# Two model blocks on one core: an extra turn at the norms' links of the branches, second buffers for bonus and gate, the first level of the inverses first, and VectorE copies over two PSUM banks

## The chip, the cores and the metric

One core of one Trainium2 chip runs the whole kernel in one launch. The metric is the device time in microseconds, the median of several runs. The engines are TensorE (PE in the profile, its weight loads PEld), VectorE (DVE), ScalarE (ACT), GpSimd (POOL) and the DMA queue of SyncE (SP). They run their own instruction streams and meet at semaphores.

## The reference, cut to what matters

Two blocks in float32 on 256 tokens of width 2048. The first block has two layers of mixed attention (stage L of the kernel). The second is one layer with a context of 256 tokens (stage P projects the inputs, stage C merges and runs the MLP). Between P and C lie the two branches, stage B, which the diff is about. Branch a is an RWKV-7 scan in both directions with 16 heads of 64, branch b a gated delta rule in both directions with 8 heads of 128.

```python
# branch a, each direction: S_t = S_{t-1} diag(w_t) - (S_{t-1} kk_t) b_t^T + v_t k_t^T ; y_t = S_t r_t
kk = l2_normalize(heads(k * k_k))
mean = jnp.mean(y, -1); var = jnp.mean(jnp.square(y - mean), -1)
out = (((y - mean) * rsqrt(var + eps)) * ln_w + ln_b + bonus) * gate     # bonus = sum_d (r k_d r_k) * v
# branch b, each direction, in chunks:
q = l2_normalize(q) * B_HEAD ** -0.5; k = l2_normalize(k)
a_mat = tril(kb @ k.T * decay, -1) + eye                                  # solved for u, w
out = o * rsqrt(mean(o * o) + eps) * norm_w * silu(gz)
```

## The kernel before, in words

Both scans are run in chunks of 128 tokens, four to a direction (the tokens of the input and of the context). A chunk needs the inverse of a unit triangular matrix. It is built by doubling: level 0 takes 2x2 blocks, level 5 blocks of 64, and a last step joins two of 64 to one of 128. X holds the inverse so far, XP its transpose, NA the matrix. A level has two links: TensorE multiplies NA by X (event `iq`), VectorE masks the result into Q; TensorE multiplies Q by XP and by itself (event `it`), and ScalarE and VectorE copy the new X and XP out of PSUM. `inverse_a` does this for eight 128-blocks (branch a, two heads by four chunks), `inverse` for four (branch b).

Stage B is a weave: eight streams (`thread_a(0)`, `thread_b(0)`, `thread_a(1)`, `thread_b(1)`, `tail_a`, `tail_b`, `base_a`, `base_b`) are generators; each engine runs its own version of all eight and takes one step, up to the next `yield`, of each in this order. One pass over the eight is a turn here. A `yield` makes no instruction: it sets only where in an engine's queue the next ones stand. Since an engine's queue is in order, a wait holds all that stands behind it. A thread's tile goes through `prep`, `scores`, the inverse and `chain` (branch a; b has its own four steps), which is 34 turns for both, eight tiles a direction. Direction 1 starts a tile when direction 0 is 8 turns into its inverse (`middle`, `middleb`). `base_a` and `base_b` prepare the next tile (mixes, convolutions, l2 norms of kk, q and k), `tail_a` and `tail_b` finish one (group norm of y and the gate; RMS norm of o).

A norm is a row of links: ScalarE squares (`sq`), TensorE sums over channels (`sums`), VectorE scales the sums (`mean`, by `ts` or `root`), GpSimd takes the power (`root`, L3226), TensorE spreads the result (`spread`), VectorE multiplies.

Lines in the profile: L574 is the `mm` helper of TensorE, L577 its transpose, L1417 and L1420 the two helpers of ScalarE (activation, copy), L2153 VectorE's `ts`. The others stand for themselves: L2734 (X and XP from the identity), L2742 (masked copies into XP), L2747 (first level of X) in `inverse_a`, L2759 its Q, L2764 and L2765 its copies; L2687 to L2703 the same in `inverse`; L2855 and L2863 the masked copies of `scores` into NA, AK, RB and RK; L2953 and L2956 thread_b's matrix, L2608 the mix for the next tile of a. PSUM is eight banks of 512 float32 a partition; branch a's direction d uses banks 2d and 2d+1 in turn (`Ring` d0, d1), the norms banks 6 and 7 (`bs`).

## Time and profile before

| | |
|---|---|
| median of 3 runs | 3774.3 us (3773.59 to 3777.36) |
| profiled execution | 3773.41 us, span 3771.5 us |
| TensorE busy | 3575.4 us, 95% of the span |
| VectorE busy | 2224.6 us, 59% |
| ScalarE, GpSimd busy | 1521.8 us, 1651.4 us |
| mean granted TensorE clock | 0.975 |
| stage B | about 1891.5 to 2822 us |
| in it, cycle of 34 turns | 107 us |

A busy engine is one that has an instruction under way; matmuls are pipelined, and their ends are modelled. The idle time in front of an instruction is put down to what released it.

### The profile page before, as it was taken

The numbers are of one execution on the slowest core, as the hardware profiler recorded it, in microseconds if no ns is written. First come the engines' busy times: TensorE is split into PE (matmuls) and PEld (weight loads), VectorE is DVE, ScalarE is ACT, GpSimd is POOL, SyncE is SP. The second block draws the span as 40 slices with busy tenths as digits, with TensorE's granted clock in tenths as the row PEclk, the third lists the DMA queues.
The fourth block names the chain that finished last, engine by engine and source line by source line (L and its number), as shares of the span: only waits on it lengthen the run. The fifth ranks groups of instructions, "written<-read, shape, count | busy, mean of one in ns | idle before, by whom it ended". The sixth has DMA issues, their size and how long they took to land. (4 is left out here: it accounts for less than half of the span.)

```text
span 3771.5 us, 79181 instructions
## 1 busy us (share of the span) xinstructions
PE 3575.4 (95%) x33504; PEld 3118.9 (83%) x33504; DVE 2224.6 (59%) x4232; ACT 1521.8 (40%) x2753; POOL 1651.4 (44%) x1195
## 2 busy tenths in 40 slices
PE   7999998999997999999979999999979999999998
PEld 6888787888786888888868878888869898989897
DVE  4645535655536776677666677666656654445443
ACT  4444434444435432232223333333334453535353
POOL 5555455555554543333321111111116566666664
PEclk9999999999999999999989999999999999999999
DMA  6445554444344777778610000000006445455543
GB/s 229 183 168 189 186 196 156 178 179 181 146 176 168 257 268 257 252 257 292 215 40 18 24 28 29 25 24 15 3 33 254 174 179 190 179 190 180 188 180 134
DMA packets 116368, 586.83 MB, mean 156 GB/s; under 512 B 20912, under 2 KB 40368, under 8 KB 51376
## 3 DMA queue, kind: packets, MB, share of 16 engines
q1 hardware_dynamic: 116016, 581.76, 42.2%
q8 instruction: 267, 4.37, 0.5%
q14 instruction: 85, 0.70, 0.1%
HBM read 561.00 MB, written 20.71 MB: 154 GB/s over the span
## 5 line engine op out<-in xcount | busy, mean ns | idle before, releaser
L574 PE MATMUL bank<-act_L,part_L 128*128 128x512 f32 (+1 forms) x4864 | 935.4, 347 | 9.2 <-DMA cst<-in_cst 4.8
L574 PEld LDWEIGHTS bank<-act_L,part_L 128*128 128x128 f32 x4864 | 756.1, 191 | 146.4 <-issue 28.1
L574 PE MATMUL bank<-act_P,part_P 128*128 128x512 f32 (+1 forms) x3488 | 716.4, 365 | 17.5 <-POOL part_P L3221 12.6
L3221 POOL TENSOR_TENSOR part_C<-wring,part_C 128x512 fp32r<-128x512 f32 x320 | 567.8, 1783 | 362.3 <-ACT part_C L1420 362.3
L3221 POOL TENSOR_TENSOR part_L<-wring,part_L 128x512 fp32r<-128x512 f32 x304 | 526.2, 1732 | 446.1 <-ACT part_L L1420 438.2
L574 PEld LDWEIGHTS bank<-act_P,part_P 128*128 128x128 f32 x3488 | 590.3, 188 | 136.9 <-DVE arena_P L2590 16.1
L574 PE MATMUL bank<-arena_B 64*64 64x64 f32 (+2 forms) x11200 | 446.0, 237 | 51.1 <-DVE arena_B L2747 24.8
L3221 POOL TENSOR_TENSOR part_P<-wring,part_P 128x512 fp32r<-128x512 f32 x184 | 306.3, 1670 | 427.7 <-ACT part_P L1420 427.7
L1420 ACT ACTIVATE part_C<-wring 128x1024 fp32r<-128x1024 f32 x320 | 338.0, 1057 | 347.9 <-PE bank L574 345.7
L574 PE MATMUL bank<-act_Y,part_C 128*128 128x258 f32 (+1 forms) x3840 | 464.8, 283 | 9.4 <-POOL part_C L3221 9.4
L574 PEld LDWEIGHTS bank<-act_Y,part_C 128*128 128x128 f32 x3840 | 463.9, 191 | 9.8 <-issue 9.6
L574 PEld LDWEIGHTS bank<-arena_B 64*64 64x64 f32 (+2 forms) x11200 | 380.7, 147 | 103.5 <-DVE arena_B L2747 27.2
L574 PE MATMUL bank<-act_C,part_C 128*128 128x512 f32 (+1 forms) x2560 | 459.6, 340 | 0.0
L574 PEld LDWEIGHTS bank<-act_C,part_C 128*128 128x128 f32 x2560 | 391.6, 188 | 58.0
L1420 ACT ACTIVATE part_L<-wring 128x1024 fp32r<-128x1024 f32 x304 | 320.7, 1056 | 255.6 <-PE bank L574 255.0
L2167 DVE TENSOR_TENSOR part_L<-wring,part_L 128x512 fp32r<-128x512 f32 x304 | 248.2, 816 | 254.7 <-ACT part_L L1420 253.5
L2167 DVE TENSOR_TENSOR part_C<-wring,part_C 128x512 fp32r<-128x512 f32 x320 | 235.0, 734 | 252.2 <-ACT part_C L1420 245.4
L2167 DVE TENSOR_TENSOR part_P<-wring,part_P 128x512 fp32r<-128x512 f32 x184 | 170.1, 925 | 189.9 <-ACT part_P L1420 189.8
L2228 DVE SCALAR_TENSOR_TENSOR arena_P<-arena_P,mods 128x512 f32<-128x512 f32 x240 | 272.7, 1136 | 8.9 <-DMA arena_P<-in_w 5.5
L1420 ACT ACTIVATE part_P<-wring 128x1024 fp32r<-128x1024 f32 x184 | 190.9, 1051 | 153.1 <-PE bank L574 152.4
L574 PE MATMUL bank<-wring,arena_B 64*64 64x64 f32 (+3 forms) x2208 | 193.1, 254 | 7.5 <-DVE arena_B L2855 3.1
L3358 POOL COPY arena_B<-cst 128x256 f32<-128x256 f32 x80 | 33.3, 416 | 379.1 <-PE bank L574 379.1
(262 smaller groups left out, 3595.1 us busy)
## 6 DMA issues: line engine op xcount, KB each, us to landing
wring<-in_w SPq DMA_DIRECT2D x404, 1024.0 KB, 4.9
arena_P<-in_w SPq DMA_DIRECT2D x64, 1024.0 KB, 5.2
mring<-in_w SPq DMA_DIRECT2D x32, 1024.0 KB, 6.6
z_kept<-arena_P SPq DMA_DIRECT2D x34, 256.0 KB, 5.7
z_kept<-arena_P SPq DMA_DIRECT2D x58, 128.0 KB, 5.6
xT<-z_kept SPq DMA_DIRECT2D x26, 256.0 KB, 2.7
arena_C<-z_kept SPq DMA_DIRECT2D x32, 128.0 KB, 2.8
cst<-z_kept SPq DMA_DIRECT2D x24, 128.0 KB, 2.1
```

Of the source, the lines that this page charges most:

```text
L574: return e.matmul(out, lhsT, rhs, start=start, stop=stop)
L1420: return e.activation(out, a, ACT.Copy, scale=scale)
L2167: tt(wl[:, 0:4, :], wring[s % NS][:, 8 * j:8 * j + 4, :], wh[:, 0:4, :].bitcast(F32), sub).then_inc(*mark("dve_lo", "lov", stage, h))
L2228: z = ts(a, x, c, None, mult, None) if row == 0 else stt(a, x, c, a, mult, add)
L3221: e.tensor_tensor(wl[:, 4:8, :], wring[s % NS][:, 8 * j + 4:8 * j + 8, :], wh[:, 4:8, :].bitcast(F32), sub).then_inc(*mark("pool_lo", "lop ...
L3358: e.tensor_copy(region(Q[lv % 2], wd, d), same).then_inc(*mark(sem, "qf", tag, lv))
```

## The change

- All eight banks become one PSUM tensor; `banks[i]` is a slice of it, so an access may span the two banks of a direction (`two_banks(d)`).
- `scores` on VectorE: NA and AK are masked out of both banks by one copy of 128x1024 each (two of 128x512 before), RB and RK by one of 128x512 each (two of 128x256 each before).
- `inverse_a`: the order of the eight units in banks, Q and XP changes (`PLACE`, `xp`, `at`), so that VectorE's masked copy into Q is one instruction of 128x256 over two banks (two of 128x128 before). The copies of X and XP keep one bank each; at level 5 ScalarE's copy into XP is 128x256 and not 128x128.
- `inverse_a` and `inverse`: X from the identity and X's first level come first, then XP from the identity and the masked copies into it. TensorE's wait for XP at level 1 of `inverse` is dropped (`lv > 1`).
- On all four engines one `yield` more before `sums` and one before `spread` of y, one before `spread` of o, one before `sums` of q in `base_b`.
- `R.bv` and `R.gate` have two buffers, taken by tile; ScalarE's copy of the gate waits for `yg` of tile c-2, not c-1.

The diff, with the hunks left out that only add a `yield` on the other engines or move the same indices:

```diff
@@ -261,7 +261,8 @@
...
 wring_ = [sb(f"wring{i}", 2048) for i in range(3)]
-banks = [ctx.enter_context(nc.psum_tensor(f"bank{i}", [128, 512], F32))[:, :] for i in range(8)]
+psum = ctx.enter_context(nc.psum_tensor("bank", [128, 4096], F32))[:, :]
+banks = [psum[:, 512 * i:512 * i + 512] for i in range(8)]
 xT = xT_.rearrange("p (k t) -> p k t", k=16)
...
@@ -410,7 +411,9 @@
...
 R.rrk = alloc(256, ("top",))
-R.pr, R.bon, R.tp, R.s, R.bv, R.gate = [alloc(256, ("stores",)) for _ in range(6)]
+spare = alloc(512, ("top",))
+R.pr, R.bon, R.tp, R.s, bv, gate = [alloc(256, ("stores",)) for _ in range(6)]
+R.bv, R.gate = [bv, spare[:, 0:256]], [gate, spare[:, 256:512]]
 D.zr, D.sr = [D.Z["k"], D.Z["v"]], [D.S["k"], D.S["v"]]
...
@@ -551,17 +554,20 @@
...
-STRAIGHT = (slice(0, 4, 3), slice(0, 4, 2))
-CROSSED = (slice(1, 3), slice(1, 4, 2))
-
-def staying(lv):
-    return slice(0, 2) if lv < 5 else slice(0, 4, 2)
-
-def moving(lv):
-    return slice(2, 4) if lv < 5 else slice(1, 4, 2)
-
-def units(pairs):
-    return [2 * s + i for s in range(4)[pairs] for i in range(2)]
+STRAIGHT = ((0, 1), (0, 2))
+CROSSED = ((2, 3), (1, 3))
+PLACE = (0, 2, 3, 1)
+
+def two_banks(d):
+    return psum[:, 1024 * d:1024 * d + 1024].rearrange("p (b c) -> p b c", b=2)
+
+def by_side(buf, lv, wd, side):
+
+    order = "p (b i m two w) -> p b i m two w" if lv % 2 == 0 else "p (i b m two w) -> p b i m two w"
+    return buf.rearrange(order, b=2, i=2, two=2, w=wd)[:, :, :, :, side, :]
+
+def in_banks(bb, wd, side):
+    return bb[:, :, 0:256].rearrange("p b (i m two w) -> p b i m two w", i=2, two=2, w=wd)[:, :, :, :, side, :]
 GLA_LEAD, GLA_MORE = 3, 2
...
@@ -1072,37 +1078,40 @@
-    straight, crossed = units(STRAIGHT[lv % 2]), units(CROSSED[lv % 2])
-    stay, move = units(staying(lv)), units(moving(lv))
+    sides = STRAIGHT[lv % 2] + CROSSED[lv % 2]
+    stay, move = ((0, 3), (1, 2)) if lv < 5 else ((0, 2), (1, 3))
+    xp = [cols(2 * PLACE[u // 2] + u % 2) for u in range(8)]
+    at = [cols(2 * sides.index(u // 2) + u % 2) for u in range(8)]
-    b0, b1 = bank(), bank()
+    bank(), bank()
-    b0, b1 = bank(), bank()
+    bank(), bank()
...
@@ -1251,7 +1260,9 @@
...
 yield
+yield
 sums(BS, ("y", c), R.s, 2)
+yield
 yield
...
@@ -1877,8 +1894,8 @@
...
 w.wait_ge(done("gate", c))
-w.wait_ge(done("yg", c - 1)) if c else None
-cp(R.gate, b2[:, 0:256]).then_inc(*mark("act_rwkv", "free", ring.name, u2))
+w.wait_ge(done("yg", c - 2)) if c >= 2 else None
+cp(R.gate[c % 2], b2[:, 0:256]).then_inc(*mark("act_rwkv", "free", ring.name, u2))
 counts.at[("gatec", c)] = counts.last("act_rwkv")
...
@@ -2683,16 +2704,19 @@
...
     w.wait_ge(point)
-for x in (X, XP):
-    e.tensor_copy(x.rearrange("p (u s) -> p u s", u=n), bc(C("id64"), n)).then_inc(*mark(sem))
+e.tensor_copy(X.rearrange("p (u s) -> p u s", u=n), bc(C("id64"), n)).then_inc(*mark(sem))
 own(sem)
-m0 = M("xt0", d * 32, 32)[:, None, :].broadcast_to([128, n, 32])
-for h in (0, 64):
-    hs = slice(h, h + 64)
-    xv = XP[hs, :].rearrange("p (u n two) -> p u n two", u=n, two=2)[:, :, :, 1 - d]
-    nv = NA[hs, :].rearrange("p (u n two) -> p u n two", u=n, two=2)[:, :, h // 2:h // 2 + 32, 1 - d]
-    e.copy_predicated(xv, m0[hs], nv).then_inc(*mark(sem))
-counts.at[("XT", tag, 0)] = counts.last(sem)
+
+def mirror():
+    e.tensor_copy(XP.rearrange("p (u s) -> p u s", u=n), bc(C("id64"), n)).then_inc(*mark(sem))
+    own(sem)
+    m0 = M("xt0", d * 32, 32)[:, None, :].broadcast_to([128, n, 32])
+    for h in (0, 64):
+        hs = slice(h, h + 64)
+        xv = XP[hs, :].rearrange("p (u n two) -> p u n two", u=n, two=2)[:, :, :, 1 - d]
+        nv = NA[hs, :].rearrange("p (u n two) -> p u n two", u=n, two=2)[:, :, h // 2:h // 2 + 32, 1 - d]
+        e.copy_predicated(xv, m0[hs], nv).then_inc(*mark(sem))
+    counts.at[("XT", tag, 0)] = counts.last(sem)
 for lv in range(6):
...
@@ -2702,6 +2726,7 @@
...
 counts.at[("X", tag, 0)] = counts.last(sem)
+mirror()
 yield
...
@@ -2730,41 +2755,44 @@
...
     w.wait_ge(point)
-for x in (X, XP):
-    e.tensor_copy(x.rearrange("p (u s) -> p u s", u=8), bc(C("id64"), 8)).then_inc(*mark(V))
+e.tensor_copy(X.rearrange("p (u s) -> p u s", u=8), bc(C("id64"), 8)).then_inc(*mark(V))
 own(V)
-for h in range(2):
-    hs = slice(64 * h, 64 * h + 64)
-    nv = NA[hs, :].rearrange("p (s u n two) -> p s u n two", s=4, u=2, two=2)[:, :, :, 32 * h:32 * h + 32, 1 - d]
-    m0 = M("xt0", d * 32, 32)[hs, None, None, :].broadcast_to([64, 2, 2, 32])
-    for out, which in ((hs, STRAIGHT[1]), (slice(64 - 64 * h, 128 - 64 * h), CROSSED[1])):
-        xv = XP[out, :].rearrange("p (s u n two) -> p s u n two", s=4, u=2, two=2)[:, which, :, :, 1 - d]
-        e.copy_predicated(xv, m0, nv[:, which]).then_inc(*mark(V))
-counts.at[("XT", tag, 0)] = counts.last(V)
 b, u = ring.take()
...
 counts.at[("X", tag, 0)] = counts.last(V)
+e.tensor_copy(XP.rearrange("p (u s) -> p u s", u=8), bc(C("id64"), 8)).then_inc(*mark(V))
+own(V)
+for h in range(2):
+    hs, away = slice(64 * h, 64 * h + 64), slice(64 - 64 * h, 128 - 64 * h)
+    nv = NA[hs, :].rearrange("p (s u n two) -> p s u n two", s=4, u=2, two=2)[:, :, :, 32 * h:32 * h + 32, 1 - d]
+    m0 = M("xt0", d * 32, 32)[hs, None, None, :].broadcast_to([64, 2, 2, 32])
+    home, gone = [XP[o, :].rearrange("p (s u n two) -> p s u n two", s=4, u=2, two=2)[:, :, :, :, 1 - d] for o in (hs, away)]
+    e.copy_predicated(home[:, 0:4:3], m0, nv[:, 0:4:2]).then_inc(*mark(V))
+    e.copy_predicated(gone[:, 1:3], m0, nv[:, 3:0:-2]).then_inc(*mark(V))
+counts.at[("XT", tag, 0)] = counts.last(V)
 yield
...
     wd = 1 << lv
-    mk = M("lev2", (d * 6 + lv) * 64, 64).rearrange("p (m w) -> p m w", w=wd)[:, None, :, :].broadcast_to([128, 2, 64 // wd, wd])
-    q = pairs(Q[lv % 2], 4, wd, d)
-    use = [ring.take(), ring.take()]
+    mk = M("lev2", (d * 6 + lv) * 64, 64).rearrange("p (m w) -> p m w", w=wd)[:, None, None, :, :].broadcast_to([128, 2, 2, 64 // wd, wd])
+    (_, u), (_, v) = ring.take(), ring.take()
     w.wait_ge(done("iq", tag, lv))
     w.wait_ge(done("qf", tag, lv - 2))
-    for (b, u), which in zip(use, (STRAIGHT, CROSSED)):
-        e.copy_predicated(q[:, which[lv % 2]], mk, pairs(b[:, 0:256], 2, wd, d)).then_inc(*mark(V, "free", ring.name, u))
-    counts.at[("Q", tag, lv)] = counts.last(V)
-    yield
-    _, (b, u) = ring.take(), ring.take()
+    e.copy_predicated(by_side(Q[lv % 2], 0, wd, d), mk, in_banks(two_banks(d), wd, d)).then_inc(*mark(V, "Q", tag, lv))
+    counts.at[("free", ring.name, u)] = counts.at[("free", ring.name, v)] = counts.last(V)
+    yield
+    use = [ring.take(), ring.take()]
     w.wait_ge(done("it", tag, lv))
-    e.tensor_copy(pairs(X, 4, wd, d)[:, CROSSED[lv % 2]], pairs(b[:, 0:256], 2, wd, d)).then_inc(*mark(V, "Xc", tag, lv))
-    e.tensor_copy(XP.rearrange("p (s c) -> p s c", s=4)[:, moving(lv)], b[:, 256:512].rearrange("p (s c) -> p s c", s=2)).then_inc(
-        *mark(V, "free", ring.name, u))
-    counts.at[("XTm", tag, lv)] = counts.last(V)
+    e.tensor_copy(by_side(X, lv, wd, d)[:, 1], in_banks(two_banks(d), wd, d)[:, 1]).then_inc(*mark(V, "Xc", tag, lv))
+    moved = ring.bufs[1][:, 256:512]
+    if lv < 5:
+        t = e.tensor_copy(XP[:, 256:512], moved)
+    else:
+        t = e.tensor_copy(XP.rearrange("p (i b c) -> p b i c", i=2, b=2)[:, 1], moved.rearrange("p (i c) -> p i c", i=2))
+    t.then_inc(*mark(V, "XTm", tag, lv))
+    counts.at[("free", ring.name, [u for b, u in use if b is ring.bufs[1]][0])] = counts.last(V)
     yield
...
@@ -2851,19 +2879,21 @@
...
     w.wait_ge(done("rz", d))
-    for k, (b, u) in enumerate(use):
-        e.copy_predicated(dst[:, 512 * k:512 * k + 512].rearrange("p (u t) -> p u t", u=4), bc(sm, 4),
-                          b.rearrange("p (u t) -> p u t", u=4)).then_inc(*mark(V, "free", ring.name, u))
-    counts.at[("NA", (c, d)) if nm == "NA" else ("AK", c, d)] = counts.last(V)
+    assert use[0][0] is ring.bufs[0]
+    e.copy_predicated(dst.rearrange("p (u t) -> p u t", u=8), bc(sm, 8),
+                      psum[:, 1024 * d:1024 * d + 1024].rearrange("p (u t) -> p u t", u=8)).then_inc(
+        *mark(V, *(("NA", (c, d)) if nm == "NA" else ("AK", c, d))))
+    for b, u in use:
+        counts.at[("free", ring.name, u)] = counts.last(V)
 use = [ring.take(), ring.take()]
...
 w.wait_ge(done("sR", c, d))
-for k, (b, u) in enumerate(use):
-    for j, dst in enumerate((g.RB, g.RK)):
-        t = e.copy_predicated(dst[:, 256 * k:256 * k + 256].rearrange("p (u t) -> p u t", u=2), bc(im, 2),
-                              b[:, 256 * j:256 * j + 256].rearrange("p (u t) -> p u t", u=2))
-    t.then_inc(*mark(V, "free", ring.name, u))
-counts.at[("RK", c, d)] = counts.last(V)
+for j, dst in enumerate((g.RB, g.RK)):
+    t = e.copy_predicated(dst.rearrange("p (k u t) -> p k u t", k=2, u=2), bc(im, 4).rearrange("p (k u) t -> p k u t", k=2),
+                          two_banks(d)[:, :, 256 * j:256 * j + 256].rearrange("p k (u t) -> p k u t", u=2))
+t.then_inc(*mark(V, "RK", c, d))
+for b, u in use:
+    counts.at[("free", ring.name, u)] = counts.last(V)
 w.wait_ge(done("cr", c - 1, d, 3)) if c else None
...
```

## Rows read from the trace of the kernel before

**Rows 1.** Page, section 1 and the VectorE digits of section 2 (40 slices of the span).

```profile
PE 3575.4 (95%) x33504; PEld 3118.9 (83%) x33504; DVE 2224.6 (59%) x4232; ACT 1521.8 (40%) x2753; POOL 1651.4 (44%) x1195
...
DVE  4645535655536776677666677666656654445443
```

**Rows 2.** Slices of the stage: length, busy us and count per engine, clock, DMA, GB/s.

```profile
1891.50:2009.00 117.50, 89.80 (x1783) 77.75 (x1783) 84.32 (x206) 36.18 (x99) 27.56 (x43) 0.84 0.15 42
2545.00:2652.00 107.00, 97.71 (x1985) 85.90 (x1985) 76.69 (x206) 40.72 (x122) 17.38 (x31) 0.96 0.05 14
2759.00:2822.00 63.00, 50.47 (x1006) 43.48 (x1006) 24.04 (x76) 19.78 (x66) 6.25 (x14) 0.93 0.02 4
```

**Rows 3.** Waits of TensorE from 1860 to 2810 us: total, times, longest.

```profile
PE bank L574 <- DVE arena_B L2747: 24.8, 15, 1.9
...
PE bank L574 <- POOL smalls L3226: 10.4, 12, 0.9
...
PE bank L574 <- ACT wring L1417: 6.7, 9, 1.8
...
PE bank L574 <- ACT arena_B L1417: 3.2, 7, 0.5
PE bank L574 <- DVE arena_B L2703: 3.2, 8, 1.2
```

**Rows 4.** Timeline, first level of direction 0: start, us, instructions, idle before.

```profile
2254.94 1.15 PE L574 MATMUL bank<-cst,arena_B 64*64 64x64 f32 x32
...
2255.43 0.69 DVE L2734 COPY arena_B<-cst 128x512 f32<-128x512 f32 x2
...
2256.16 1.85 DVE L2742 COPY_PREDICATED arena_B<-msk,arena_B 64x128 f32<-64x128 uint8 x4
...
2258.04 0.72 DVE L2747 COPY_PREDICATED arena_B<-msk,bank 128x256 f32<-128x256 uint8 x1
...
2258.82 0.69 PE L574 MATMUL bank<-arena_B 64*64 64x64 f32 x32 [1.87 <-DVE arena_B L2747]
...
2259.58 0.73 DVE L2759 COPY_PREDICATED arena_B<-msk,bank 128x128 f32<-128x128 uint8 x2 [0.70 <-PE bank L574]
```

**Rows 5.** Timeline, first level of direction 1, VectorE and TensorE.

```profile
2312.74 1.08 DVE L2953 SCALAR_TENSOR_TENSOR arena_B<-arena_B,cst,bank 128x128 f32<-128x128 f32 x4
...
2312.99 0.69 PE L574 MATMUL bank<-arena_B 64*64 64x64 f32 x32 [1.56 <-DVE arena_B L2747]
...
2315.22 0.66 PE L577 MATMUL bank<-cst,arena_B 128*128 128x128 f32 x4 [0.18 <-DVE arena_B L2608]
```

**Rows 6.** Groups by form, VectorE, stage B: busy us, mean ns, idle before.

```profile
L2759 DVE COPY_PREDICATED arena_B<-msk,bank 128x128 f32<-128x128 uint8 x160 | 43.0, 325 | 41.0 <-PE bank L574 41.0
L2855 DVE COPY_PREDICATED arena_B<-msk,bank 128x512 f32<-128x512 uint8 x64 | 42.8, 720 | 38.2 <-PE bank L574 38.2
...
L2863 DVE COPY_PREDICATED arena_B<-msk,bank 128x256 f32<-128x256 uint8 x64 | 23.0, 438 | 12.8 <-PE bank L574 12.8
...
L2747 DVE COPY_PREDICATED arena_B<-msk,bank 128x256 f32<-128x256 uint8 x16 | 11.5, 722 | 0.5
...
L2703 DVE COPY_PREDICATED arena_B<-msk,bank 128x128 f32<-128x128 uint8 x16 | 7.1, 442 | 0.5
```

**Rows 7.** Slices around the norm of y, and those of q and k.

```profile
2280.05:2295.80 15.75, 14.32 (x273) 12.37 (x272) 13.70 (x35) 6.71 (x19) 4.28 (x6) 0.89 0.03 5
2333.60:2343.05 9.45, 7.91 (x193) 6.05 (x184) 9.00 (x23) 4.46 (x12) 1.50 (x3) 0.97 0.23 71
```

**Rows 8.** Timeline, TensorE, the spread of y's norm.

```profile
2288.58 0.66 PE L574 MATMUL bank<-cst,smalls 128*64 128x128 f32 x8 [0.91 <-POOL smalls L3226]
```

**Rows 9.** Slices of 3.15 us, one turn each.

```profile
2311.55:2314.70 3.15, 1.52 (x39) 1.38 (x40) 3.09 (x11) 0.42 (x1) 0.00 (x0) 1.00 0.43 119
2314.70:2317.85 3.15, 2.97 (x43) 2.71 (x45) 1.53 (x5) 2.44 (x8) 0.90 (x1) 1.00 0.41 124
2343.05:2346.20 3.15, 3.15 (x43) 2.92 (x46) 1.33 (x8) 0.00 (x0) 1.01 (x1) 0.50 0.03 5
```

More of the change, by code:

```diff
@@ L1023, in inverse @@
                     w.wait_ge(done("X", tag, lv - 1))
-                    w.wait_ge(done("XT", tag, lv - 1)) if one else None
+                    w.wait_ge(done("XT", tag, lv - 1)) if one and lv > 1 else None
                     diagonal(b, NA, X, True).then_inc(*mark("pe_inv", "iq", tag, lv))
@@ L1357, in tail_b @@
                     sums(BS, ("o", h), G.so, 1)
+                    yield
                     yield
@@ L1832, in inverse_a @@
                     yield
-                    (b, u), _ = ring.take(), ring.take()
+                    use = [ring.take(), ring.take()]
                     wd = 1 << lv
                     w.wait_ge(done("it", tag, lv))
-                    cp(pairs(X, 4, wd, d)[:, STRAIGHT[lv % 2]], pairs(b[:, 0:256], 2, wd, d)).then_inc(*mark(V, "X", tag, lv))
-                    cp(pairs(XP, 4, wd, 1 - d)[:, staying(lv)], pairs(b[:, 256:512], 2, wd, 1 - d)).then_inc(*mark(V, "free", ring.name, u))
-                    counts.at[("XT", tag, lv)] = counts.last(V)
+                    cp(by_side(X, lv, wd, d)[:, 0], in_banks(two_banks(d), wd, d)[:, 0]).then_inc(*mark(V, "X", tag, lv))
+                    if lv < 5:
+                        t = cp(pairs(XP[:, 0:256], 2, wd, 1 - d), pairs(ring.bufs[0][:, 256:512], 2, wd, 1 - d))
+                    else:
+                        t = cp(XP.rearrange("p (i b c) -> p b i c", i=2, b=2)[:, 0], ring.bufs[0][:, 256:512].rearrange("p (i c) -> p i c", i=2))
+                    t.then_inc(*mark(V, "XT", tag, lv))
+                    counts.at[("free", ring.name, [u for b, u in use if b is ring.bufs[0]][0])] = counts.last(V)
                     yield
@@ L1956, in tail_a @@
                     yield
+                    yield
                     BS.take()
+                    yield
                     yield
@@ L2054, in tail_b @@
                     BS.take()
+                    yield
                     yield
@@ L2912, in tail_a @@
                     yield
+                    yield
                     b, u = BS.take()
@@ L2923, in tail_a @@
                     own(V)
-                    tt(y, y, R.bv, add).then_inc(*mark(V))
+                    tt(y, y, R.bv[c % 2], add).then_inc(*mark(V))
                     own(V)
                     w.wait_ge(done("gatec", c))
-                    tt(y, y, R.gate, mult).then_inc(*mark(V, "yg", c))
+                    tt(y, y, R.gate[c % 2], mult).then_inc(*mark(V, "yg", c))
                     yield
@@ L3390, in tail_a @@
                     yield
+                    yield
                     root(("y", c), small(3), 4)
+                    yield
                     yield
@@ L3429, in base_b @@
                     yield
+                    yield
                     root(("q", h), small(4), 2)
```

29 lines of the change are left out of this document (19 added, 10 removed).

## Prediction, made before the changed kernel was run

> **What bounds the kernel now.** I read the page first, then slices of time, then the waits of one stage, then single instructions. The page [rows 1] shows TensorE busy for 95% of the span and VectorE for 59%, but from the middle on the VectorE digits stand at 6 and 7. The whole diff lies in the branches (stage B), from about 1891.5 us to 2822 us, so the rest of the span should not move. There the work repeats: thread_a and thread_b both take 34 turns of the weave for one tile (prep 5, scores 4, inverse 13, chain 12; for b 4, 13, 12 and PAD 5), and the trace repeats every 107 us, which is 3.15 us a turn. Of the 107 us of one such cycle [rows 2] TensorE is busy 97.7 and VectorE 76.7; the six from 2009 us to 2652 us are alike. So TensorE is the bound on average, and stands for some 9 us a cycle, 70 us in the stage. That is the most that any reordering can win, before the clock.
>
> The waits of TensorE in this stage [rows 3] say what it stands for. The largest is L2747, the masked copy that makes the first level of X in `inverse_a`: 24.8 us in 15 waits. Then come the norms' links: POOL's roots (10.4), ScalarE's squares for q and k (6.7) and for y (3.2). L2703, the same first-level copy of `inverse`, has 3.2 us.
>
> **First level first.** In the instance of direction 0 [rows 4] TensorE has written the first product (instruction of 32 matmuls at 2254.94, done at 2256.09). VectorE makes X and XP from the identity (0.69 for both), runs four masked copies for XP (1.85), and only then L2747 (0.72). TensorE was ready at 2258.82 - 1.87 = 2256.95. In the new order X(0) is there at 2255.43 + at most 0.5 + 0.72 = 2256.65, before TensorE asks: the whole 1.87 us wait goes. But VectorE's sum doesn't shrink. It still owes XP and its masked copies (2.35 us) and is free at about 2259.05, and the next link, Q of level 1 (L2759 at 2259.58, which had waited for the product), can't go earlier than that. What is won is TensorE's product hidden behind XP's copies: 2259.58 - 2259.05 = 0.5, and up to 0.8 with Q in one instruction. I take 0.8 of the 1.87.
>
> In direction 1 [rows 5] L2953, which masks thread_b's matrix (1.08 us), follows L2747 on VectorE, then the mix for base_a (L2608), and TensorE waits for all three: 1.56 + 0.19 + 0.18. With the new order alone the product would run early, and TensorE would stand for L2953 at the same 2313.8. But base_b(0) now takes one turn more before it says "baseb", so that thread_b is one turn behind thread_a for the whole stage (counted over the streams: b's inverse of direction 1 begins in turn 97 and not 96, a's stays in turn 94 to 95). L2953 leaves the crowded turn, and L2608 comes about 1.0 earlier. I take 0.9. Over 15 waits: 15 x 0.85 = 13 us. Bounds: 0 (VectorE is the limit all the way) and 24.8 (all waits). For L2703, whose mirror copies move behind it too, and whose TensorE wait for XT is dropped at level 1: 2 of 3.2 us.
>
> **One more turn at the norms' links.** The yields go into the same places of all engines' streams: sums y, spread y, spread o, and the sums of q and k. They make no work. Waits that stand at these links: 10.4 + 6.7 + 3.2 = 20.3 us at most. An instance is the spread of y [rows 8], which waits 0.91 for a root. Yet both places are crowded on VectorE [rows 7]: busy 13.70 of 15.75 us around y, where TensorE has 14.32, and 9.00 of 9.45 around q and k. So the stretches can shrink by no more than 15.75 - 14.32 = 1.4 and 9.45 - 9.00 = 0.45 in a cycle, 8 x 1.9 = 15 us, and where VectorE is the cover TensorE will wait for something else on it. I take half: 8 us. What the yields cost: cycles stay 34 turns, since base_b is ready in turn 27 or 28 of 34 and tail_a ends far before the next Y. The stage has 298 turns for 297 by the same count: one turn at the start, in which little but chains of dependent work runs, at most one turn of 3.15 us; I take 2 us lost. Queued behind a late `yg` would have been ScalarE's gate copy, and behind it a's scores; the second buffers of `bv` and `gate` cover just that, and cost no instruction. They are worth 0, and without them the gate copy (turn 22 of a cycle) would wait for `yg` (now turn 23).
>
> **Two banks in one copy.** Instructions removed on VectorE: 80 of L2759 (two of 128x128 become one of 128x256), 32 of L2855 (two of 128x512 become one of 128x1024), 32 of L2863 (four of 128x256 become two of 128x512) [rows 6]. Consecutive copies overlap: a pair of L2759 covers 43.0/80 = 0.54 us, and one of 256 elements takes 0.438 by L2863's row: 0.1 saved, 8 us in all. A pair of L2855 covers 42.8/32 = 1.34; the slope from 256 to 512 elements is 282/256 = 1.10 ns, so 1024 take 0.720 + 0.563 = 1.28: 2 us. Four of L2863 cover 23.0/16 = 1.44, two of 512 about 1.34: 2 us. That is 12 us of VectorE, in a stage where it is mostly not the last: a third counts, 4 us, bounds 0 and 12. The traffic of ScalarE and VectorE with the banks doesn't change: for X and XP each still reads one bank, and only VectorE spans two. At level 5 ScalarE copies 128x256 for 128x128, beside other work, 0.
> The Trainium skill's page "VectorE: DVE Perf Modes", section "The TRN2 errata", charges every VectorE read of PSUM 120 cycles at 0.96 GHz beyond its elements, so an instruction removed would be worth 0.125 us. By it 144 instructions are an estimated 18 us and not 12, and the third would be 6 and not 4. The overlap of pairs in the rows of this trace speaks for the smaller one.
>
> **Sum.** 3773.4 (this execution: span 3771.5 and 1.9 around it) - 13 - 2 - 8 - 4 + 2 = 3748.4. The median of the three runs is 0.9 higher, so I forecast 3749, 0.67% less.
>
> **Rivals.**
> (a) It goes further: every wait named is won and the clock holds. The granted clock is 0.96 over a cycle [rows 2]; a slice with TensorE busy throughout shows 0.50, the lower level of 1.2 GHz, right behind the stretch of q's and k's norms in which it stood for 1.5 us [rows 7, 9], while the slice at 2311.55, busy for only 1.52 of 3.15, keeps 1.00 and so does the next [rows 9]. 0.04 of 107 us means 8.6 us a cycle at the half level, which costs at most 4.3 us a cycle, 34 in all. With 8 us of that, 20 from the first level, 12 from the links and 6 from the copies: 3774 - 3 - 8 - 20 - 12 - 6 + 2 = about 3727 (the 3 are L2703's). For it: the dips follow the links that get a turn. Against: VectorE is the cover there. The Trainium skill, "TensorE: Matmul & The Clock Gate", section "What's actually happening", has the clock gate follow recent activity, so fewer waits would mean fewer dips; the second of these slices shows that a wait alone doesn't bring one.
> (b) The waits only change their name: TensorE leaves L2747 and stands for L2759 and L2953, the links' waits go to VectorE's prep and conv. Then the lines give 4 us, the copies 4, the turn costs 2: about 3768; with a little of the first level 3760. For it: VectorE is busy for 3.09 of 3.15 us in the slice of the instance in rows 5 [rows 9], and the shift by one turn puts the scaling of k beside a's last prep step, which was full. Against: in the next slice it is busy for only 1.53 [rows 9], so that there is room for what is put off.
> (c) Slower: the masked copies over two banks run at the rate of L2747 (722 ns for 256 elements with a step of two) and not at that of L2863 (438). Then Q costs 80 x (0.72 - 0.54) = 14 us more, NA and AK (2.4 for 1.34) 34, RK 18: 66 us of VectorE. Half of it on the path is 33: 3774 - 25 + 4 + 33 = 3786. It decides from about 29 us on the path, and could be measured from 37. Against: L2759, whose runs are 2 to 32 elements long, takes 325 ns for 128 elements, and L2703, with a step of two, 442 [rows 6]; the new patterns keep the runs.
> (d) That the change doesn't do what it says: the links' extra turn shows no shorter waits since a root comes in the turn of its sum, as before, and only the reader moves. That is inside (b).
>
> **Chances and range.** Forecast (3738 to 3760) 0.60; (a) 0.15; (b) and (d) 0.18; (c) 0.07. A change of 0.2%, 7.5 us, is about what a measurement of this kernel can tell from none. Faster takes the forecast, (a) and some 0.07 of (b): 0.82. Within 0.2% takes 0.11 of (b) and 0.02 of (c): 0.13. Slower: 0.05. The range 3728 to 3766 leaves out half of (a)'s far side, the end of (b) and all of (c), 2 in 10.
>
> **What the changed profile would show.** Right: TensorE's wait for the first-level copy is gone from the stage's list (under 3 us), the cycle is 104 us and not 107, VectorE's sum in the stage is 8 to 14 us less, and no wait for POOL's roots at y and o. In the turn after the first level I expect a new wait of about 1 us for Q or for base_a's mix. Wrong: a cycle of 107 us with the same TensorE idle time under other names (b), a two-bank copy of 128x256 at over 0.6 us (c), or a mean clock of 0.98 and more with a cycle under 102 us (a). Outside 1891 to 2822 us nothing should move; if it does, I have missed a part.

## The result: 36 us slower, and the profile after

The changed kernel takes 3810.9 us in the median (3809.8 to 3811.5), the one before 3774.4 (3773.6 to 3777.4): ratio 1.0095, 95% interval 1.0077 to 1.0112. I had forecast 3749. The profiled execution has a span of 3808.9 us. Of all runs below, one execution of before_filled was in the slow state (7013.6 us) and counts in no ratio.

The page of the changed kernel, its first rows (to hold against [rows 1]):

```profile
PE 3599.4 (94%) x33504; PEld 3142.9 (83%) x33504; DVE 2224.5 (58%) x4088; ACT 1533.3 (40%) x2753; POOL 1646.3 (43%) x1195
...
PE   7999999999998999999888898999998999999998
...
DVE  5646535555436776677666666666657654445443
```

VectorE has the 144 instructions less, as counted, yet the same busy time; TensorE has the same number with 24 us more of busy time. Up to 1880 us nothing moved (TensorE is busy 1804.1 us there before and 1804.6 after); the loss lies in stage B. Each first-level copy of a direction comes once a cycle, so two of them that lie six cycles apart give slices that can be compared. Before (length, then busy us with counts for PE, PEld, DVE, ACT, POOL, then clock, DMA, GB/s):

```profile
2035.03:2705.14 670.11, 615.53 (x12624) 543.01 (x12624) 473.05 (x1272) 254.77 (x762) 116.32 (x198) 0.96 0.07 21
```

And after:

```profile
2036.10:2742.55 706.45, 636.69 (x12626) 563.50 (x12625) 470.77 (x1165) 264.98 (x762) 112.70 (x198) 0.92 0.07 20
```

A cycle is 670.11/6 = 111.7 us before and 117.7 after. (My prediction has 107 us, and 3.15 for a turn: it did not measure between two like instructions; a turn is 3.29.) Six cycles lose 36.3 us, which is the whole result but for 1.1 us lost ahead of them. Of that, 15.2 is TensorE standing longer (54.6 to 69.8), and 21.2 is more busy time for the same matmuls, at a granted clock of 0.92 and not 0.96. The second part is the larger one, and my sum had no term for it.

TensorE's waits of the changed kernel in stage B, 1860 to 2850 us (total, times, longest; to hold against [rows 3]):

```profile
PE bank L580 <- ACT arena_B L1433: 38.8, 24, 3.1
PE bank L583 <- DVE arena_B L2629: 15.4, 7, 2.2
PE bank L580 <- DVE arena_B L3015: 14.9, 7, 2.2
...
PE bank L580 <- DVE arena_B L2783: 8.3, 8, 1.1
PE bank L580 <- DVE arena_B L3007: 6.1, 6, 1.1
```

The first-level copy, GpSimd's roots and ScalarE's squares are gone from it, as forecast. In their place: ScalarE's copies (L1433, the copy helper), the mix for base_a (L2629, L2608 before), the update of thread_b's state (L3015), Q (L2783). Here is ScalarE ahead of the first of them:

```profile
2298.90 0.71 ACT L1433 ACTIVATE arena_B<-bank 128x128 f32<-128x128 f32 x3
2301.40 1.15 ACT L1430 ACTIVATE arena_B<-arena_B 128x512 f32<-128x512 f32 x2 [1.80 <-DVE arena_B L2838]
2302.46 0.40 ACT L1430 ACTIVATE wring<-arena_B 128x256 f32<-128x256 f32 x1
...
2303.14 0.59 ACT L1433 ACTIVATE arena_B<-bank 64x512 f32<-64x512 f32 x1
```

TensorE stands 2.38 us to 2303.78 for the last row, a copy of 0.59 us whose product had been there since 2300.88. ScalarE's queue is in order, and ahead of the copy stand the exponentials of direction 1's prep, which wait 1.80 us for VectorE. And VectorE in the first-level turn of direction 1 (to hold against [rows 5]):

```profile
2325.56 0.73 DVE L2763 COPY_PREDICATED arena_B<-msk,bank 128x256 f32<-128x256 uint8 x1
2326.09 0.45 DVE L2766 COPY arena_B<-cst 128x512 f32<-128x512 f32 x1
2326.57 1.21 DVE L2773 COPY_PREDICATED arena_B<-msk,arena_B 64x128 f32<-64x128 uint8 x1
2327.81 0.69 DVE L2774 COPY_PREDICATED arena_B<-msk,arena_B 64x128 f32<-64x128 uint8 x1
...
2329.47 0.75 DVE L2174 TENSOR_SCALAR arena_B<-arena_B,par 128x512 f32<-128x512 f32 x2
2330.14 0.74 DVE L2629 SCALAR_TENSOR_TENSOR arena_B<-xT,par,arena_B 128x512 f32<-128x512 f32 x1
2330.80 0.28 DVE L2740 COPY arena_B<-bank 128x128 f32<-128x128 f32 x1
2331.00 0.72 DVE L2783 COPY_PREDICATED arena_B<-msk,bank 128x256 f32<-128x256 uint8 x1
```

X(0) comes early, but XP's work (3.4 us with two slow copies) stands between it and the mix (L2629), for which TensorE stands 2.19 us.

### The profile page after: what moved, and what is told of

The parts are those of the page before. It is cut to its first block, busy times and chain, and to the rows that moved or that the text cites. A ratio compares the mean times of both kernels' runs of the same rounds, so it can differ in the third digit from the quotient of the medians.

```text
span 3808.9 us, 79014 instructions
## 1 busy us (share of the span) xinstructions
PE 3599.4 (94%) x33504; PEld 3142.9 (83%) x33504; DVE 2224.5 (58%) x4088; ACT 1533.3 (40%) x2753; POOL 1646.3 (43%) x1195
## 4 chain that ended last, share of the span: by engine, by line
PE 84%; DVE 9%; ACT 3%; issue 2%; POOL 1%; DMA 0%; DVEq 0%; SPq 0%; POOLq 0%; ACTq 0%
PE bank L580 82%; PE bank L583 1%; ACT part_P L1433 1%; POOL act_L L3296 1%; DVE part_P L2188 1%; DVE act_P L2588 1%; ACT part_L L1433 1%; DVE arena_B L2174 1%; POOL part_L L3255 0%; DVE arena_B L2892 0%; DVE arena_L L2174 0%; ACT arena_B L1430 0%; DVE xT L2525 0%; DVE arena_B L2836 0%; ACT arena_L L1433 0%
## 5 line engine op out<-in xcount | busy, mean ns | idle before, releaser
L580 PE MATMUL bank<-arena_B 64*64 64x64 f32 (+4 forms) x11200 | 457.4, 239 | 73.3 <-ACT arena_B L1433 38.8
L580 PEld LDWEIGHTS bank<-arena_B 64*64 64x64 f32 (+3 forms) x11200 | 389.3, 149 | 128.8 <-ACT arena_B L1433 42.0
L1433 ACT ACTIVATE part_C<-wring 128x1024 fp32r<-128x1024 f32 x320 | 337.9, 1057 | 344.8 <-PE bank L580 341.3
L1433 ACT ACTIVATE part_L<-wring 128x1024 fp32r<-128x1024 f32 x304 | 320.7, 1056 | 254.9 <-PE bank L580 254.5
L1433 ACT ACTIVATE part_P<-wring 128x1024 fp32r<-128x1024 f32 x184 | 191.0, 1051 | 153.1 <-PE bank L580 152.5
L1433 ACT ACTIVATE arena_B<-bank 128x128 f32<-128x128 f32 (+4 forms) x376 | 120.4, 350 | 232.6 <-PE bank L580 118.4
L580 PE MATMUL bank<-wring,arena_B 64*64 64x64 f32 (+3 forms) x2208 | 202.4, 263 | 3.9 <-DVE arena_B L2883 1.9
```

The costliest lines, as they stand in the source:

```text
L580: return e.matmul(out, lhsT, rhs, start=start, stop=stop)
L1433: return e.activation(out, a, ACT.Copy, scale=scale)
```

## The experiments

All ratios are to the kernel before, from runs on the same chip. Cycle, idle time and clock are those of six cycles between like first-level copies, in the one execution that was profiled. For two_banks that one took 3765.0 us, 8 us over the median: its nine times spread from 3753.7 to 3767.0. The ten of base_turn_kept are six of 3774.0 to 3777.9 and four of 3797.9 to 3799.4. The columns of these two kernels are to be read with that in mind.

| run | median us | ratio (95%) | cycle us | TensorE idle in it | clock |
|---|---|---|---|---|---|
| before | 3774.4 | 1 | 111.7 | 9.1 | 0.96 |
| the change | 3810.9 | 1.0095 (1.0077, 1.0112) | 117.7 | 11.6 | 0.92 |
| shift_alone | 3808.7 | 1.0093 (1.0076, 1.0110) | 117.8 | 10.6 | 0.91 |
| shift_undone | 3784.9 | 1.0031 (1.0019, 1.0043) | 114.9 | 8.5 | 0.92 |
| no_turns | 3763.4 | 0.9978 (0.9969, 0.9988) | 111.6 | 7.9 | 0.95 |
| tail_turns | 3780.9 | 1.0023 (1.0014, 1.0033) | 113.2 | 9.4 | 0.95 |
| two_banks | 3756.9 | 0.9960 (0.9950, 0.9971) | 111.5 | 8.3 | 0.95 |
| first_alone | 3769.0 | 0.9987 (0.9978, 0.9996) | 112.4 | 8.4 | 0.94 |
| base_turn_kept | 3777.0 | 1.0030 (1.0010, 1.0050) | 112.7 | 9.6 | 0.95 |
| before_filled | 3780.3 | 1.0013 (1.0004, 1.0023) | 113.0 | 3.9 | 0.98 |
| no_turns_filled | 3747.5 | 0.9926 (0.9910, 0.9943) | 109.3 | 3.9 | 1.00 |
| changed_filled | 3823.2 | 1.0129 (1.0114, 1.0144) | 119.5 | 7.3 | 0.96 |
| changed_filled_less | 3792.3 | 1.0048 (1.0031, 1.0065) | 116.2 | 6.9 | 0.93 |
| two_banks_filled | 3745.0 | 0.9925 (0.9910, 0.9940) | 108.2 | 4.5 | 0.99 |
| no_turns_filled_less | 3740.4 | 0.9907 (0.9892, 0.9922) | 107.9 | 4.8 | 0.99 |
| b_one_earlier | 3800.8 | 1.0066 (1.0051, 1.0081) | 116.2 | 12.8 | 0.95 |
| b_two_later | 3860.0 | 1.0224 (1.0207, 1.0242) | 123.0 | 14.2 | 0.90 |
| shift_late_a | 3775.7 | 1.0002 (0.9993, 1.0011) | 112.3 | 9.3 | 0.95 |
| changed_late_a | 3791.0 | 1.0045 (1.0028, 1.0062) | 115.9 | 10.8 | 0.93 |

### Which part costs

`FIRST_B` is the number of turns that base_b lets pass before its first tile, and `LATE_A` the number that base_a lets pass before each of its tiles. **shift_alone** is the kernel before with one constant:

```
-        LATE_A, LATE_B, LATE_TA, LATE_TB, FIRST_B = 2, 3, 0, 0, 4
+        LATE_A, LATE_B, LATE_TA, LATE_TB, FIRST_B = 2, 3, 0, 0, 5
```

> The kernel before with one edit: the constant FIRST_B is 5 and not 4, so that every base_b(0) says its word one turn later and thread_b stands one turn behind where it stood against thread_a, for the whole of the branches. No work changes. Theory A (the change is slower because of this shift, which the extra turn of base_b brings with it: ScalarE's copies of a's inverse fall behind b's or a's exponentials, b's state update falls behind a's first level): 3795 to 3815 us, with TensorE's waits for ScalarE's copy of arena B and for the update of b's state in its list. Theory B (the shift is harmless, and the loss comes from the order with the first level first or from the copies over two banks): within 8 us of 3774. My forecast had the shift as a help to L2953's turn: by it 3762 to 3774.

**shift_undone** is the changed kernel with `FIRST_B` at 3.

> The changed kernel with FIRST_B at 3 and not 4: base_b keeps its extra turn between conv and norms, but thread_b stands against thread_a as in the kernel before. Theory A (the shift costs the time): 3745 to 3770 us, that is the other parts bring what they were forecast to bring. Theory B (order or copies cost it): 3800 to 3815, as the changed kernel.

**no_turns** takes out of the changed kernel every added `yield`:

```
 base_b  -                    yield      (before sums of q)
 tail_a  -                    yield      (before sums of y, before spread of y)
 tail_b  -                    yield      (before spread of o)
```

> The changed kernel without any of the extra turns (base_b, tail_a, tail_b): the first level first and the copies over two banks are left, and the second buffers. Theory A (the shift costs the time): 3750 to 3770 us (17 to 19 less than before by my sum without the links' 8 and the turn's 2). Theory B (the new order or the copies cost it): over 3790. A rival to both: the turns at y and o cost it, then this kernel too stands under 3775.

**tail_turns** is the kernel before with those of tail_a and tail_b, and the second buffers.

> The kernel before with the extra turns of tail_a (sums y, spread y) and of tail_b (spread o) and the second buffers of bv and gate alone; no turn in base_b, the old order, copies of one bank. Theory A (only the shift of thread_b costs): 3766 to 3775 us, the links' 8 us at best. Theory C (yg and its followers now fall into turns in which VectorE is full, and TensorE waits for what stands behind them): 3780 to 3800.

The constant alone, with no instruction changed, costs what the whole change costs: 3808.7. Its six cycles:

```profile
2032.89:2739.61 706.72, 642.89 (x12624) 570.86 (x12624) 478.46 (x1273) 263.17 (x762) 109.04 (x198) 0.91 0.07 20
```

Of its 36.6 us over the row of before, 9.2 are idle time and 27.4 busy time for exactly as many matmuls. Its waits in stage B, 1860 to 2850 us:

```profile
PE bank L574 <- DVE arena_B L2747: 35.5, 15, 2.8
PE bank L574 <- ACT arena_B L1420: 22.5, 23, 3.4
```

Before, L2747 stood at 24.8 (longest 1.9) and ScalarE's copies at 6.2 in 8 waits. Theory A holds, but not to the end. Undoing the shift wins 26 us back in the changed kernel, so most of the loss is the shift's there too; but 3784.9 is left and not 3745 to 3770, because the turns in themselves cost (tail_turns, 8 us), where I had expected 8 us won. Without any turn the change is faster than before, by 0.22%.

### The parts one by one

**two_banks** is no_turns with VectorE's old order; **first_alone** is the kernel before with the new one (`inverse_a`, and the like in `inverse`):

```
-                for x in (X, XP):
-                    e.tensor_copy(x..., bc(C("id64"), 8))
+                e.tensor_copy(X..., bc(C("id64"), 8))
+                (first level: L2747)
+                e.tensor_copy(XP..., bc(C("id64"), 8))
                 (masked copies into XP)
```

> The kernel before with the copies over two banks (and the second buffers), but the first level behind XP's copies as before, and no extra turn. no_turns has both and stands at 3763.4, 9 us under before. By my sum the copies give 4 and the first level 15, so this one: 3766 to 3771 us, with the waits for the first-level copy (24.8 us) still there. If the first level is a gain only in name (its waits went to thread_b's matrix, 12.6 us, and the clock fell from 0.96 to 0.95), this kernel stands at no_turns' time or under it: 3758 to 3764.

> The kernel before with the first level ahead of XP's copies, in inverse_a and inverse, and nothing else. My forecast had 15 us won by it. By the runs so far it is worth less than nothing: copies over two banks without it have ratio 0.9960, with it 0.9978. If the parts add: 1.0018, 3778 to 3784 us, with the waits for X gone, waits for thread_b's matrix in their place, and a granted clock in the cycle of 0.94 or 0.95 for 0.96. If it helps when alone: under 3770.

**base_turn_kept** is the kernel before with the turn of base_b and `FIRST_B` at 3, so that thread_b stays.

> The kernel before with the extra turn of base_b between its convolutions and the norms of q and k, and FIRST_B at 3, so that thread_b stands where it stood. Sums of the runs so far: the changed kernel with the shift undone has ratio 1.0031, without any turn 0.9978, and the turns at y and o alone 1.0023; what is left for base_b's turn is 1.0031 - 0.9978 - 0.0023 = 0.0030, or 11 us. If the parts add, this kernel has 3780 to 3788 us. If the parts don't add (the turn costs only in the changed order of VectorE), 3770 to 3776.

The copies over two banks give 0.40%, the best single part (the second buffers are in it too), and more than either range that I gave for it. The first level first gives 0.13% by itself, and on top of the copies it seems to take 0.18% away (0.9960 to 0.9978, where the intervals touch, so that this sign isn't certain): it is not my 15 us, nor a loss in itself. base_b's turn costs 0.30% by the ratio, 3 us by the medians and 6 us by six cycles. The ratio is carried by the four long executions, so the size is uncertain. The parts add for shift_undone: 0.9978, 1.0023 and 1.0030 make 1.0031, as measured. With the shift's 1.0093 they would give 1.012 for the whole change, where 1.0095 was measured; that the collisions overlap would explain it, but isn't shown.

### Is it the wait, or the clock behind it?

The fillers are matmuls into the bank that was just taken, ahead of the wait; the products that follow overwrite them, so the result stays. In before_filled (the two ahead of the spread of y are left out here):

```
+            def fill(out, n):
+                for _ in range(n):
+                    mm(out, ident, C("scan"), True, True)
...
+                    b0 = bank()
+                    fill(b0, 4) if lv == 1 else None
                     w.wait_ge(done("X", tag, lv - 1))
```

> The kernel before, with matmuls that nobody reads put where TensorE stands: four of 128x512 into the bank that was just taken, ahead of the wait for X at level 1 of inverse_a (15 waits of 1.56 to 1.87 us), and two ahead of the spread of y (0.91 us). No result changes. Before has 9.1 us of idle TensorE in a cycle of 111.7 us and a granted clock of 0.96. Clock theory (a stand costs less by itself than by the half clock that follows it): the clock rises to 0.98 or more where the filled waits were followed by a dip, and the kernel is 5 to 25 us faster, though TensorE has more work. Idle theory (a wait costs its own length and no more): 3773 to 3785 us, since filling a wait wins nothing and the fillers outlast some of the waits.

> The changed kernel without extra turns (3763 us, clock 0.95 over six cycles, idle 7.9 us a cycle) with fillers of 128x512: four at level 1 of direction 1 only, where the wait has moved to thread_b's next product (1.55 us), two ahead of the spread of y, one each ahead of the sums of y and q. In its cycle the clock is at the half level for some 3 us behind the waits at y and for some 7 behind that of thread_b. Clock theory: 3735 to 3758 us and a clock of 0.98 or more. Idle theory: 3763 to 3775.

> The changed kernel (3811 us) with fillers of 128x512 where it stands longest: six ahead of the last product of inverse_a in direction 0 (waits of 2.4 to 2.6 us for ScalarE's copy of X), five ahead of base_a's transposes (2.19 us for L2629). Nothing else differs. Clock theory (27 of the 36 us that the changed kernel lost are TensorE's half clock, 9 are idle time): two of its three dips a cycle go, 3780 to 3800 us. Idle theory: 3811 to 3830.

The clock rose in all three, but two of the three times (3780.3 and 3823.2) fell into the range of the idle theory; only no_turns_filled, 16 us faster than no_turns, came out as the clock theory has it. One of these expectations has a wrong attribution: 27 and 9 us are shift_alone's; for the changed kernel they are 21 and 15. And the fillers were far too long: each is issued as two matmul instructions and takes 0.9 us. Slices of 3 us of the changed kernel, from the copy before the wait for ScalarE on (columns as above):

```profile
2298.46:2301.46 3.00, 2.78 (x46) 2.37 (x42) 2.90 (x10) 1.09 (x5) 0.92 (x2) 1.00 0.02 5
2301.46:2304.46 3.00, 0.68 (x6) 0.68 (x7) 2.90 (x8) 2.88 (x7) 0.10 (x1) 0.68 0.00 0
2304.46:2307.46 3.00, 3.00 (x46) 2.88 (x45) 1.15 (x4) 0.42 (x1) 1.31 (x2) 0.50 0.00 0
2307.46:2310.46 3.00, 3.00 (x15) 2.53 (x15) 2.27 (x5) 1.04 (x3) 0.12 (x2) 0.68 0.00 0
```

The same stretch in changed_filled, where it begins at 2307.14:

```profile
2307.14:2310.14 3.00, 3.00 (x47) 2.59 (x44) 2.90 (x10) 1.08 (x5) 0.91 (x2) 1.00 0.02 5
2310.14:2313.14 3.00, 3.00 (x8) 1.33 (x7) 2.90 (x8) 2.88 (x7) 0.09 (x1) 1.00 0.00 0
2313.14:2316.14 3.00, 3.00 (x31) 1.66 (x31) 0.15 (x1) 0.42 (x1) 1.02 (x1) 1.00 0.00 0
2316.14:2319.14 3.00, 3.00 (x44) 2.78 (x39) 2.82 (x6) 1.04 (x3) 0.29 (x1) 1.00 0.00 0
```

The PE column of the second slice shows the stand (0.68 of 3.00), and the clock column falls in it and stays at the half level in the next. With the filler the clock stays at 1.00. The matmuls behind the stand in the timeline of the changed kernel (start, length):

```profile
2303.78 1.65 PE L580 MATMUL bank<-arena_B 64*64 64x64 f32 x13 [2.38 <-ACT arena_B L1433]
...
2307.03 1.22 PE L580 MATMUL bank<-arena_B,cst 128*128 128x256 f32 x2
2308.04 1.69 PE L580 MATMUL bank<-xT,arena_B 128*128 128x256 f32 x4
2309.57 0.50 PE L580 MATMUL bank<-cst,wring 128*128 128x1 f32 x4
```

And the filler with the same matmuls in changed_filled:

```profile
2309.72 5.40 PE L580 MATMUL bank<-cst 128*128 128x512 f32 x12
2315.05 0.97 PE L580 MATMUL bank<-arena_B 64*64 64x64 f32 x13
...
2316.88 0.70 PE L580 MATMUL bank<-arena_B,cst 128*128 128x256 f32 x2
2317.42 1.03 PE L580 MATMUL bank<-xT,arena_B 128*128 128x256 f32 x4
2318.28 0.50 PE L580 MATMUL bank<-cst,wring 128*128 128x1 f32 x4
```

From the end of the wait to the matmuls of 128x1 it takes 5.79 us at the half clock (2303.78 to 2309.57) and 3.23 at the full one (2315.05 to 2318.28). So a stand of 2.38 us cost 2.56 more behind it. The overlong filler (5.40 us) made the 13 matmuls behind it start 7.91 us after the first copy of the stretch, where they had started at 5.32: 2.59 later, so this stretch came out even. That the overshoot was on the path elsewhere would explain the longer times, and three kernels with fillers of 128x256 at half the length try it:

```
-                    mm(out, ident, C("scan"), True, True)
+                    mm(out[:, 0:256], ident, C("Sm"), True, True)
```

> The changed kernel with shorter fillers. In the run with six and five fillers of 128x512 these took 5.4 us for a wait of 2.4, and the stretch from that wait to the next tile's scores was as long as without them (17.39 us for 17.36), with the clock at 1.00 for 0.80: what the filler took beyond the wait was what the half clock had cost. Here five and four fillers of 128x256, at 0.45 us each 2.2 and 1.8 us, just under the waits. Clock theory: the overshoot goes and the gain stays, 2.5 to 3.5 us a cycle in direction 0 and 0.5 to 1 at base_a's transposes: 3775 to 3795 us for the changed kernel's 3811. Idle theory: 3805 to 3815.

> The copies over two banks (3757 us) with fillers of 128x256: two and three ahead of X at level 1 of inverse_a in direction 0 and 1 (waits of 1.35 and 1.29 us, the second followed by some 9 us at the half level), one ahead of the sums of y and of q, two ahead of the spread of y. Clock 0.95 in its cycles of 111.5 us, that is some 11 us at the half level and up to 5.5 us lost in each. Clock theory: 3715 to 3740 us, which beats both kernels. Idle theory: 3757 to 3765.

> The changed kernel without extra turns (3763 us) with fillers of 128x256 for 128x512: three ahead of X at level 1 of direction 1, two ahead of the spread of y, one ahead of the sums of y and of q. The longer ones gave 3747 and took some 3.7 us for a wait of 1.55. If what they took beyond the wait was on the path: 3730 to 3742 us. If it lay in slack (VectorE, last there, was not done earlier): 3744 to 3750.

The changed kernel wins 19 us with nothing but idle work in two of its waits (9 of them in the six cycles), the kernel with the copies alone 12, and the one with copies and new order (no_turns) 23, of which 7 came from shortening the fillers:

```profile
2025.31:2672.53 647.22, 618.40 (x12710) 537.45 (x12709) 466.62 (x1165) 255.55 (x762) 117.08 (x198) 0.99 0.08 22
```

Six cycles take 22.2 us less than in no_turns, with more matmuls in them. TensorE's idle time falls by 18.4 us, about what the 42 fillers take (six instructions, three fillers, cover 1.56 us in this trace: an estimated 20 us or so), and its busy time falls by 3.8 although the fillers are in it. So the gain is in the time of the other matmuls, at a clock of 0.99 for 0.95. An idle theory can't have that: a filler makes no product arrive sooner. This version, at 3740.4 us, is the fastest of all and beats both kernels (0.93% under before). The forecasts for the fillers' sizes were off: two_banks_filled missed its 3715 to 3740. So did the attempt on the kernel before: with fillers of 128x512 it is 0.13% slower, and shorter ones were not tried there.

### Why one turn costs so much

**b_one_earlier** and **b_two_later** are the kernel before with `FIRST_B` 3 and 6, **shift_late_a** has `FIRST_B` 5 and `LATE_A` 3 for 2, and **changed_late_a** is the changed kernel with `LATE_A` 3.

> The kernel before with FIRST_B at 3: thread_b stands one turn before where it stood against thread_a (295 turns in all). Whether the old place is a good one by itself: if any other place costs (the shift by one later cost 36 us), 3785 to 3815 us with new waits of 2 us and more; if it is only the place one turn later that is bad, since there thread_b's state update and GpSimd's masks meet a's first level and ScalarE's copies meet the exponentials of prep, 3765 to 3778 us.

> The kernel before with FIRST_B at 6, thread_b two turns behind its old place (298 turns). If the place one turn later is bad for its own collisions: 3765 to 3790 us. If the loss grows with the distance (because base_b's work then meets more of prep): 3815 to 3850.

> The shift alone (FIRST_B 5, 3809 us) and LATE_A at 3 for 2, so that base_a, whose mixes and transposes meet VectorE's masked copies of the first level in direction 1, comes one turn later too. In the shift alone TensorE stands 2.8 us at that place and the clock is at the half level for 10 us behind it. If that collision is a main part of the 36 us: 3785 to 3797. If the loss is spread over the ScalarE copies and the rest: 3803 to 3815.

> The changed kernel with LATE_A at 3 for 2: base_a comes one turn later too, and stands against thread_b as in the kernel before. With the shift alone this won 33 us back (3809 to 3776). The changed kernel stood 2.19 us a cycle for base_a's mix (L2629), which should go, and with it the half clock behind it. If the change is slower only because base_a was left in its place: 3765 to 3785 us. If ScalarE's copy behind the exponentials and the update of thread_b's state (2.4 and 2.2 us a cycle) cost by themselves: 3790 to 3808.

The old place is a good one and both sides of it are worse: +25 us one turn earlier, +35 one later, +84 two later. (By the count that gives 297 turns before, these two kernels have 296 and 299, not 295 and 298.) When base_a moves with thread_b, all of it comes back (1.0093 to 1.0002), more than either expectation allowed. The waits of shift_late_a, 1860 to 2850 us:

```profile
PE bank L574 <- DVE arena_B L2747: 24.4, 15, 2.1
PE bank L574 <- ACT arena_B L1420: 22.8, 23, 3.4
```

TensorE stands as long for ScalarE's copies as in shift_alone (22.8 and 22.5), but L2747 is back near its old 24.8. This speaks against ScalarE's copies, which theory A had named too, and for the stand at the first level, in the turn in which VectorE also has base_a's mix (L2608). One such place, in shift_alone and then in shift_late_a, in slices of 3 us:

```profile
2326.01:2329.01 3.00, 1.22 (x36) 1.15 (x37) 2.91 (x8) 0.97 (x3) 0.03 (x1) 0.97 0.46 118
2329.01:2332.01 3.00, 3.00 (x17) 3.00 (x15) 2.00 (x8) 2.31 (x7) 0.00 (x0) 0.50 0.34 73
2332.01:2335.01 3.00, 3.00 (x40) 2.88 (x43) 0.17 (x1) 0.36 (x2) 1.97 (x2) 0.50 0.41 123
2335.01:2338.01 3.00, 3.00 (x60) 2.88 (x54) 0.62 (x2) 1.16 (x4) 0.42 (x1) 0.50 0.13 39
...
2307.59:2310.59 3.00, 1.77 (x57) 1.56 (x53) 2.97 (x7) 0.27 (x2) 1.64 (x4) 1.00 0.02 7
2310.59:2313.59 3.00, 3.00 (x87) 2.87 (x86) 2.87 (x11) 2.22 (x7) 0.49 (x2) 1.00 0.31 80
```

TensorE stands 2.82 us and has the half clock for some 10 us behind it; with base_a moved it stands 1.23 and the clock stays. One rival is open: no kernel has LATE_A at 3 and nothing else, so a gain that base_a's later turn brings by itself can't be told from the place against thread_b.

In the changed kernel the same constant wins 20 back (the waits for L2629 are gone from its list, ScalarE's have 43.6 us and L3015 14.9). That is the second of my two ranges: 0.45% stay above before. They may be these two waits, or what the turns of tail_a, tail_b and base_b cost (0.23% + 0.30% = 20 us) less what no_turns wins (8); no run separates the two.

## Why the prediction was wrong

The step that failed is the one in "First level first" that takes the shift of thread_b as a help: "L2953 leaves the crowded turn, and L2608 comes about 1.0 earlier. I take 0.9." I had seen the shift and counted it right (b's inverse of direction 1 begins in turn 97 and not 96), but followed it to two instructions. It moved all of thread_b, base_b and tail_b on four engines. Where the step had 0.9 us won at each such wait, the shift by itself (shift_alone) brought +36 us; in the changed kernel, undoing it wins 26 back.

- First level first, -13 and -2: the waits for L2747 and L2703 went, as forecast. One reading of rows 4 was wrong: X's first level reads the product that TensorE has done at 2256.09, so X(0) is there at 2256.09 + 0.72 = 2256.81 at the earliest and not at 2256.65, still ahead of TensorE. In the changed kernel VectorE waits for that product (7.0 us in 16 instances). first_alone shows what came in their place, 2.01 us for thread_b's matrix in direction 1 with some 7 us of half clock behind it: -5 us alone, and by the ratios +7 beside the copies. This is rival (b), "the waits only change their name".
- Norm links, -8: in tail_turns the roots' waits went (1.0 us left of 13.8, 1860 to 2850 us), but TensorE then stood for ScalarE's squares, 17.4 us where there were 6.7. The turns cost 8 us (y and o) and, with the uncertainty above, 3 to 11 (q and k). The sign was wrong.
- Copies, -4 on the path of 12 saved: mis-sized. These rows of the changed kernel (to hold against [rows 6]) save 3.7, 1.1 and 1.7 = 6.5 us of VectorE, yet two_banks is 15 us faster. Rival (c) falls: 491 ns for 128x256, not 720. The sign that I named for this part, VectorE's sum 8 to 14 us less, isn't there: the page has 2224.5 for 2224.6, since the masked copies that run beside GpSimd's masks (below) take back about what is saved, 1.0 us in each of eight turns.

```profile
L2883 DVE COPY_PREDICATED arena_B<-msk,bank 128x1024 f32<-128x1024 uint8 x32 | 41.7, 1304 | 30.9 <-PE bank L580 30.9
L2783 DVE COPY_PREDICATED arena_B<-msk,bank 128x256 f32<-128x256 uint8 x80 | 39.3, 491 | 17.6 <-PE bank L580 16.5
L2892 DVE COPY_PREDICATED arena_B<-msk,bank 128x512 f32<-128x512 uint8 x32 | 21.3, 720 | 12.4 <-PE bank L580 12.4
```

- The turn at the start, +2: the weave has 298 turns for 297, as counted, and the second tile's first-level copy stands 1.1 us later (2036.10 for 2035.03). This term was of the right size.
- The clock: I had it as a rival's bonus, at most 34 us, and in no term of the sum. TensorE's added busy time was 21 of the 36 us. "The second of these slices shows that a wait alone doesn't bring one" was true of a slice and misled me: the same wait of 1.56 us in direction 1 ([rows 5]) is followed by no dip in one cycle and by a dip in the next one, in these slices of the kernel before:

```profile
2312.21:2315.21 3.00, 1.85 (x40) 1.53 (x40) 3.00 (x10) 0.92 (x3) 0.00 (x0) 1.00 0.47 127
2424.44:2427.44 3.00, 3.00 (x42) 2.88 (x36) 2.71 (x10) 1.71 (x5) 0.00 (x0) 0.50 0.20 53
```

Not settled: why two_banks wins more (15 us) than the time it saves on VectorE, and which collision on ScalarE or VectorE makes b_two_later so slow (3860 us, where my expectation ended at 3850). Nor was a place for base_a tried by itself or beside each part.

## What to carry to other kernels

In streams that are woven by turns, a turn added to one stream moves everything behind it against every other stream; test the bare shift first (one constant, no instruction), and look for a stream that has to move with it. Where TensorE is near its bound, price a wait at its length plus the half-clock time behind it, which doubled the one of 2.38 us, and where a wait can't be removed, try to fill it with matmuls that nobody reads, no longer than the wait (12 to 23 us won in three kernels here; overlong ones lost 6 and 12 in two of three). Measure a cycle between two like instructions.
